# A gated-delta layer's head preparation: query scaling, query products and convolution rows one chunk later, absolute values on ScalarE

## What is computed

```python
qkv, new_buf = _causal_conv(qkv, buf, conv_w)       # 4 taps, then silu
q = _l2norm(q) * (GDN_DK ** -0.5)
k = _l2norm(k)
# per chunk: M = I + strict(beta * k k^T * decay), u and w by M^-1
Aqk = jnp.einsum('nbhtk,nbhsk->nbhts', q, k) * decay
def step(S, inp):
    v_new = uc - jnp.einsum('bhtk,bhkv->bhtv', wc, S)
    o = einsum(qc, S) + einsum(ac, v_new)
    S = glc[..., None, None] * S + jnp.einsum('bhsk,bhkv->bhkv', kc, v_new)
o = _rmsnorm(o, out_norm) * jax.nn.silu(g)           # g is z in the kernel
```

## Time and profile before

| | |
|---|---|
| median of 3 runs | 2057.86 us (2053.31 to 2070.72) |
| the profiled execution | 2055.79 us, its span 2054.0 us |
| busy: PE, PEld | 1845.4 us (90%), 1746.1 us (85%) |
| busy: DVE, ACT, POOL | 1142.2 us (56%), 530.3 us (26%), 543.7 us (26%) |
| mean granted clock of PE | 0.922 of full speed |
| chain that ended last | PE 42%, DVE 5%, ACT 4% of the span; L489 28% |
| GDN heads 0 to 7 | about 977 to 1600 us of the span |

### The profile page before, as it was taken

How to read it: one execution, slowest core, us unless ns; L and a number is a source line. 1 busy time by engine, 2 the same in 40 slices (tenths; PEclk the granted TensorE clock), 3 DMA queues, 4 the chain that set the end, 5 groups by cost and what they waited for, 6 DMA issues and landing times.

```text
span 2054.0 us, 34009 instructions
## 1 busy us (share of the span) xinstructions
PE 1845.4 (90%) x13227; PEld 1746.1 (85%) x13227; DVE 1142.2 (56%) x1824; ACT 530.3 (26%) x991; POOL 543.7 (26%) x303
## 2 busy tenths in 40 slices
PE   3999999979999999977988888888978899999997
PEld 3988888869999999976877778777757899999996
DVE  5677777758625252766456555556542771616263
ACT  1544445421000000114334434434421110100011
POOL 1100000006656565641000000000000565656562
PEclk9989999989999999987988988999966999999997
DMA  5122222212323222221120120120110223232321
GB/s 167 52 63 63 63 67 68 63 55 83 93 83 93 82 84 84 83 63 26 50 65 22 44 64 20 44 64 21 43 44 1 84 83 92 84 90 84 89 84 43
DMA packets 257434, 135.99 MB, mean 66 GB/s; under 512 B 6698, under 2 KB 255876, under 8 KB 257348
## 3 DMA queue, kind: packets, MB, share of 16 engines
q1 hardware_dynamic: 219700, 114.03, 19.5%
q10 hardware_dynamic: 37648, 20.68, 3.5%
HBM read 122.70 MB, written 12.00 MB: 66 GB/s over the span
## 4 chain that ended last, share of the span: by engine, by line
PE 42%; DVE 5%; ACT 4%; issue 3%; ACTq 0%; POOL 0%; DVEq 0%; POOLq 0%
PE pj L489 28%; PE rr L527 3%; PE rr L763 2%; PE rr L739 2%; PE rr L510 1%; DVE pr L1607 1%; PE rr L755 1%; PE rr L748 1%; PE rr L832 1%; PE rr L820 1%; PE rr L684 1%; DVE ol L1824 1%; ACT ws L1086 1%; ACT w_hi L945 1%; ACT ng L1079 1%
## 5 line engine op out<-in xcount | busy, mean ns | idle before, releaser
L450 POOL TENSOR_SCALAR w_hi<-w_raw 128x1024 fp32r<-128x1024 f32 x149 | 157.3, 1056 | 1464.2 <-PE pj L489 1433.4
L489 PE MATMUL pj<-xh,w_hi 128*128 128x272 f32 x2064 | 472.5, 311 | 23.4 <-DVE xl L1372 9.1
L489 PE MATMUL pj<-xh,w_lo 128*128 128x272 f32 x2064 | 443.7, 298 | 0.0
L489 PE MATMUL pj<-xl,w_hi 128*128 128x272 f32 x2064 | 443.4, 298 | 0.0
L452 POOL TENSOR_TENSOR w_lo<-w_raw,w_hi 128x1024 fp32r<-128x1024 f32 x149 | 386.1, 2591 | 12.5
L489 PEld LDWEIGHTS pj<-xh,w_hi 128*128 128x128 f32 x2064 | 339.4, 199 | 47.1 <-issue 23.9
L489 PEld LDWEIGHTS pj<-xl,w_hi 128*128 128x128 f32 x2064 | 341.9, 198 | 4.0 <-issue 4.0
L489 PEld LDWEIGHTS pj<-xh,w_lo 128*128 128x128 f32 x2064 | 340.3, 198 | 0.0
L489 PE MATMUL pj<-oh,w_hi 128*128 128x272 f32 x1280 | 271.1, 293 | 16.9 <-DVE ol L1402 5.4
L489 PE MATMUL pj<-oh,w_lo 128*128 128x272 f32 x1280 | 267.0, 290 | 0.0
L489 PE MATMUL pj<-ol,w_hi 128*128 128x272 f32 x1280 | 266.7, 290 | 0.0
(11 more groups left out here) (273 smaller groups left out, 2279.6 us busy)
## 6 DMA issues: line engine op xcount, KB each, us to landing
w_raw<-in_mlp_w_up_dram SPq DMA_DIRECT2D x64, 512.0 KB, 4.0
w_raw<-in_mlp_w_down_dram SPq DMA_DIRECT2D x64, 512.0 KB, 3.7
w_raw<-in_hgrn_w_in_dram SPq DMA_DIRECT2D x32, 512.0 KB, 4.0
w_raw<-in_gdn_w_in_dram SPq DMA_DIRECT2D x32, 512.0 KB, 4.2
out_dram<-S ACTq DMA_DIRECT2D x16, 512.0 KB, 3.3
S<-in_state_hgrn_dram ACTq DMA_DIRECT2D x8, 512.0 KB, 4.0
w_raw<-in_hgrn_w_out_dram SPq DMA_DIRECT2D x8, 512.0 KB, 3.7
S<-in_state_gdn_dram ACTq DMA_DIRECT2D x8, 512.0 KB, 4.2
```

The lines of the kernel that those rows point to most:

```text
L450: nc.gpsimd.tensor_scalar(w_hi[:, s], w_raw[:, j], 1.0, 1.0, ALU.mult, ALU.mult).then_inc(hi_pool, 1)
L489: last = mm(pj[:, s, b, 0:HALF], w[:, s, k, :], v[:, k, b * HALF:(b + 1) * HALF], start=(k == 0 and a == 0), stop=(k == KT - 1 and a == 2))
```

## The change

In program order on each engine:

- DVE loses the four `negative_abs` of a head. ACT's `soft` takes the convolved rows themselves and makes three activations of them, `Abs`, `Exp` with scale −1, and `Ln`.
- DVE: `nl` moves from C2 to C0, `qn` from C0 to C1 (behind z's evacuation), `qkd` from C1 to a new slot C3, which runs after the last state. `low(U_GIN+5)` moves from c = 0 to c = 1.
- ACT: `high(U_GIN+5)` moves from c = 0 to c = 1, behind z's exponential and logarithm; `zsig` stays in C2; `cout` and the stores move to C3, behind the copy and the square of the output (`oo`, `sq`), with `high(U_GIN+6)` behind them.
- PE: `qk` moves from C1 to C2, `stash` from C2 to C3, behind `dSs0` and two tiles. One of the three last tiles moves ahead of `gdn_first_inverse`.

```diff
-                if slot == "C1":
+                if slot == "C2":
                     pe.wait_ge(v.sem, v.after("qn", h))
                     for c in range(NC):
                         cols = slice(c * P, (c + 1) * P)
                         mm(rr[:, 2 + c // 2, c % 2 * P:(c % 2 + 1) * P], nK[:, cols], nQ[:, cols], start=True, stop=True)
                     t.did(mm(rr[0:TS, 3, 2 * P:2 * P + TS], nK[:, TP:T], nQ[:, TP:T], start=True, stop=True), "qk")
-                if slot == "C2":
+                if slot == "C3":
                     held((v, "qkd", h))
...
-                    if nxt is not None:
+                    if nxt is not None and c < NC - 1:
                         gdn_prepare(f"C{c}", nxt)
                 pe.wait_ge(v.sem, v.after("S3", h))
                 t.did(mm(rr[:, 0, :], kdTs[:], gd_vbig[0], start=True, stop=True), "dSs0")
                 later(2)
                 if nxt is not None:
+                    gdn_prepare("C3", nxt)
+                    later(1)
                     pe.wait_ge(s.sem, s.after("oo", h))
                     gdn_first_inverse(nxt, (sa, "cout", nxt))
                 pe.wait_ge(v.sem, v.after("sn0", h))
                 t.did(mm(rr[:, 0, :], kdTs[:], gd_vbig[1], start=True, stop=True), "dSs1")
-                later(3)
+                later(2)
...
-            def soft(row, w, exp, ln):
+            def soft(name, row, w, h):
 
                 s = st["ga"][1]
-                s.did(f(ng[:, row, 0:w], ng[:, row, 0:w], ACT.Exp), exp[0])
-                sem_of(s, *exp)
-                s.did(f(ng[:, row, 0:w], ng[:, row, 0:w], ACT.Ln, bias=1.0), ln)
+                s.did(f(ng[:, row, 0:w], pr[:, row, 0:w], ACT.Abs), f"{name}abs")
+                sem_of(s, f"{name}abs", h)
+                s.did(f(ng[:, row, 0:w], ng[:, row, 0:w], ACT.Exp, scale=-1.0), f"{name}exp")
+                sem_of(s, f"{name}exp", h)
+                s.did(f(ng[:, row, 0:w], ng[:, row, 0:w], ACT.Ln, bias=1.0), f"{name}ln")
...
-                    sem_of(v, "qneg", h)
-                    soft(1, YW, ("qexp", h), "qln")
+                    sem_of(v, "q3", h)
+                    soft("q", 1, YW, h)
...
-                    sem_of(v, "zneg", h)
-                    soft(2, T, ("zexp", h), "zln")
+                    act.wait_ge(unit_out, h * 4 + (U_GIN + 3 + 3))
+                    soft("z", 2, T, h)
                 if slot == "C2":
+                    sem_of(v, "zls", h)
+                    s.did(f(ng[:, 2, 0:T], ng[:, 2, 0:T], ACT.Exp), "zsig")
+                if slot == "C3":
...
-                    sem_of(v, "zls", h)
-                    s.did(f(ng[:, 2, 0:T], ng[:, 2, 0:T], ACT.Exp), "zsig")
...
-                    if nxt is not None:
+                    if nxt is not None and c < NC - 1:
                         gdn_prepare(f"C{c}", nxt)
-                        if c == 0:
+                        if c == 1:
                             high(nxt, U_GIN + 5)
-                        if c == NC - 1 and not final:
-                            high(nxt, U_GIN + 6)
                 sem_of(t, "o", h)
                 s.did(f(oo[:, 0:TP], rr[:, 1, :], ACT.Copy), "oo")
                 sem_of(s, "oo", h)
                 s.did(f(sqr, oo, ACT.Square), "sq")
+                if nxt is not None:
+                    gdn_prepare("C3", nxt)
+                    if not final:
+                        high(nxt, U_GIN + 6)
...
-                    after(v, f"{name}3", h)
-                    v.did(negative_abs(row, YW), f"{name}neg")
...
-                    after(s, "rnq", h)
-                    v.did(stt(out=nQ, in0=nQ, scalar=float(P) ** -0.5, in1=G, op0=ALU.mult, op1=ALU.mult), "qn")
-                if slot == "C1":
-                    tt(halves(pr[:, 2, 0:T]), computed(U_GIN, h * 4, 3), halves(rstd[:]), ALU.mult).then_inc(unit_out, 1)
-                    dve.wait_ge(unit_out, h * 4 + (U_GIN + 3 + 3))
-                    v.did(negative_abs(2, T), "zneg")
-                    after(t, "qk", h)
-                    decayed(3, "qkd")
-                if slot == "C2":
                     after(v, "kkd", h)
                     tt(blocks(gd["NL"][:, 0:TP], P), blocks(work[:, 0:TP], P), over_chunks(cf[:, C_NSTR:C_NSTR + P]), ALU.mult)
                     v.did(tt(gd["NL"][0:TS, TP:T], work[0:TS, TP:T], cf[0:TS, C_NSTRS:C_NSTRS + TS], ALU.mult), "nl")
+                if slot == "C1":
+                    tt(halves(pr[:, 2, 0:T]), computed(U_GIN, h * 4, 3), halves(rstd[:]), ALU.mult).then_inc(unit_out, 1)
+                    after(s, "rnq", h)
+                    v.did(stt(out=nQ, in0=nQ, scalar=float(P) ** -0.5, in1=G, op0=ALU.mult, op1=ALU.mult), "qn")
+                if slot == "C2":
                     after(s, "zln", h)
                     v.did(log_sigmoid(2, T), "zls")
+                if slot == "C3":
+                    after(t, "qk", h)
+                    decayed(3, "qkd")
...
-                        if c == 0:
+                        if c == 1:
                             low(nxt, U_GIN + 5)
```

More of the change, by code:

```diff
@@ L52 @@
 Q_ROW, K_ROW, V_ROW = 0, 1, 2
-GDN_SLOTS = ["L0", "L1", "L2x", "L2", "L3x", "L3", "L4x", "L4", "L5x", "L5", "L6x", "L6", "C0", "C1", "C2"]
+GDN_SLOTS = ["L0", "L1", "L2x", "L2", "L3x", "L3", "L4x", "L4", "L5x", "L5", "L6x", "L6", "C0", "C1", "C2", "C3"]
 SRT = 352
@@ L236, in build @@
             gp=["x", "neg", "ls", "g", "g2", "scan", "dl"],
-            ga=["cols", "gsel", "k1", "k2", "k3", "kneg", "kls", "q1", "q2", "q3", "qneg", "dec", "ks", "qls", "kn", "kb",
-                "v1", "v2", "v3", "vneg", "qs", "kkd", "vls", "vs", "qn", "zneg", "qkd", "nl", "zls", "tt0", "tt1", "A",
+            ga=["cols", "gsel", "k1", "k2", "k3", "kls", "q1", "q2", "q3", "dec", "ks", "qls", "kn", "kb",
+                "v1", "v2", "v3", "qs", "kkd", "vls", "vs", "nl", "qn", "zls", "qkd", "tt0", "tt1", "A",
                 "qe", "cols2", "nbe"],
@@ L253, in build @@
             gp=["A", "exp", "ln", "be", "el", "eg", "cols"],
-            ga=["hist", "past", "ktap", "qtap", "vhist", "kexp", "kln", "G", "ksig", "qexp", "qln", "bb", "dec",
-                "sqk", "vtap", "qsig", "lnk", "rnk", "eG", "sqq", "vexp", "vln", "vsig", "lnq", "rnq", "zexp", "zln", "cout",
-                "zsig", "K", "tm0"],
+            ga=["hist", "past", "ktap", "qtap", "vhist", "kabs", "kexp", "kln", "G", "ksig", "qabs", "qexp", "qln", "bb", "dec",
+                "sqk", "vtap", "qsig", "lnk", "rnk", "eG", "sqq", "vabs", "vexp", "vln", "vsig", "lnq", "rnq",
+                "zabs", "zexp", "zln", "zsig", "cout", "K", "tm0"],
             gr=["x2", "tt2", "x4", "tt4", "x8", "tt8", "x16", "tt16", "x32", "rs", "tt32", "vns", "x64", "os",
@@ L1110, in gdn_prepare @@
                 if slot == "L3":
-                    sem_of(v, "kneg", h)
-                    soft(0, YW, ("kexp", h), "kln")
+                    soft("k", 0, YW, h)
                 if slot == "L4x":
@@ L1140, in gdn_prepare @@
                 if slot == "L6":
-                    sem_of(v, "vneg", h)
-                    soft(0, YW, ("vexp", h), "vln")
+                    sem_of(v, "v3", h)
+                    soft("v", 0, YW, h)
                 if slot == "C0":
```

## The result

The changed kernel takes **2083.46 us** (median of 7 runs, 2077.59 to 2087.25) against 2064.54 us for the kernel before (7 runs beside them). The medians differ by 19 us; the ratio is 1.0106, 95% interval 1.007 to 1.0141, which makes it slower by about 22 us. The forecast was +10 us. The profiled execution took 2087.25 us (span 2085.4, mean clock 0.915; before 2055.79, 2054.0 and 0.922), 31 us more than the one of before.

What follows compares the result with a forecast made beforehand. TensorE's own work, its stalls and the half clock bound a head. Six heads at +2.2 (walk +1.5, levels +0.7) make +13.2, plus 0.35, less 3.6: +10 us on 2055.8, so 2066 us, range 2042 to 2084.

Steps and rivals of the forecast that it cites:

- rival (d): Levels' added 0.70 us brings 1.7 us more half clock in seven heads, both tiles stay half clock: 2076 to 2088, chance 0.22.
- The levels, +0.70 us per head: Absolute values on ACT: k and v cost nothing, q's delays `x32` and `dt32` by 0.70 us in seven heads.
- The walk up to dSs0: Chunks 0 to 3: `vn1` 2.2 us earlier, `vn2` 1.65 after a 3.6 us stall, `vn3` 2.36; 1.2 half clock after `vn2`.
- From dSs0 to the next head: End of the walk: `dSs1` stalls 4.4 us for `sn0`, starting at 1138.0 against 1138.44, then two tiles.
- the half clock ending inside, 4.25: After `sn0`: `dSs1` 2.0 us, one tile about half clock, 2.0 + 0.75 + 1.5 = 4.25 us, making +0.3 instead of −1.4.
- the upper bound of +3.0: Per head, with half clock through both last tiles: +1.1 + 1.2 + 0.7 = +3.0 us; +18 us over six heads.
- I take 0.6 per head off for it, −3.6: Deduction over six heads, since a head of another length than the 78.55 us ones meets the half clock elsewhere.
- Head 0's preparation, 0: Gains 0.67 (v's absolute value off DVE before `sqq`), loses 0.64 (`stash` behind a later `qkd`): 0.
- Head 6, +0.35: Head without tile or `high(U_GIN+6)`: `dSs1` 0.35 us forward, with the levels' +0.70 it is +0.35 us.
- Rival (c): ACT's two issues or DVE's order do not hold `sn0`, the 4.4 us stall falls away: 2030 to 2040, chance 0.08.

Runs made afterwards that it cites:

- the two pads: The changed kernel with idle ACT copies behind q's logarithm in every head, one of 544 columns or four of 128: 2080.39 and 2084.76 us.
- `high6_back`: The changed kernel with `high(U_GIN+6)` back in its old place on ACT, right behind the last chunk's copy: 2040.15 us.
- `both`: The changed kernel with `high(U_GIN+5)` ahead of z's three activations and `high(U_GIN+6)` back behind the last chunk's copy: 2021.39 us.
- `moves_only`: The changed kernel with all four absolute values back on DVE, the moves kept: 2080.96 us, ratio 1.0103 to the kernel before.

## Why the prediction was right in direction and too small

The measured time lies 0.5 us inside the stated range and in the interval of rival (d). The stalls came as forecast, and the sum made too little of them: one term was too small and one had the wrong sign.

**The levels, +0.70 us per head: right.** The wait before `dt32` is 1.04 us, and from the next head's first matmul behind the projections (L510) to `vn0` it takes 0.72 us longer. So k and v cost nothing, as said.

**The walk up to dSs0: right.** From `vn0` (1111.65 before, 1122.63 after), `vn1` comes 2.41 us earlier (said 2.2), `vn2` 1.61 (said 1.65), `vn3` 1.14 (said 2.36 less 1.2 of half clock, 1.16), `dSs0` 1.39 (said 2.84 less 1.2).

**From dSs0 to the next head: mis-sized, by 1.3 us a head.** `dSs1` comes 28.15 us behind `vn0` instead of 26.61, +1.54; the sum had −0.44 + 1.2 = +0.76. `cout` starts 3.27 us behind `dSs0`, where 2.8 was taken, and `dSs0` itself was 0.25 us later than said. From `cout` on it is 5.58 us against 5.7. A last 0.18 is that the old `dSs1` was read at 1138.44 in the chain, where the timeline has 1138.26. Then "the half clock ending inside, 4.25" failed: from `dSs1` to the first matmul of the next head it is 4.80 us, with `dSs1` and nearly all of the twelve matmuls at half clock. The walk is +2.8 us instead of +1.5, and a head +3.5 instead of +2.2. That is above the upper bound of +3.0, too. Six heads make +21, and the fit over all runs has +21.3 at equal half clock.

A check was at hand in the prediction's own numbers. Its stalls add up to 3.6 + 4.4 + 0.7 against 2.23 + 1.95, +4.5 us of standing in each head; with a head of +2.2 TensorE would have to be busy 2.3 us less. It was busy 0.83 us less.

**"I take 0.6 per head off for it, −3.6": wrong in sign.** I took the heads of 78.55 us for unlucky ones, which any change of length would on average help. For a pad in the kernel before that is true (−59 us of half clock). For this change it is not: the first five heads all have 18 to 21 us of half clock in the profiled execution, and the two pads win none. The two intervals which before took 74.38 and 75.90 us, with 10.4 and 13.6 us of half clock, now have 19.2 and 20.7 and take 81.44 and 82.13. Over all runs the changed kernel has 343 us of half clock against 330, so in place of −3.6 this term is about +5 (0.40 × 13 us). That the two long stalls are what keeps the half clock is argued from `high6_back` (295 us), which removes one, and `both` (277 us), which removes it and cuts the other to 1.0 us; it is not shown apart from the place of the heads.

With both put right the sum is 21 + 0.5 + 5 = 27 us, against 22 by the ratio and 31 between the profiled executions.

**Head 0's preparation, 0: +0.1. Head 6, +0.35: +0.5, in part by luck.** In head 6 `dSs1` was to come 0.35 us earlier against `vn0` and comes 1.95 earlier (21.88 us behind it, 23.83 before); 7.3 us more half clock in that interval (27.1 against 19.8), and the late end of the head before it, fill the place. The +2.8 us ahead of the heads are in no step. The same matmuls took longer there, with 10 us more half clock; the change has no part in that stretch, and runs of one kernel differ by more.

**The rivals.** The time fell into (d)'s interval, and the second half of (d) came true: both tiles stay at half clock nearly to the end, 0.55 us above the 4.25 of the sum. The reason that (d) gave first didn't. The extra half clock lies in the heads that had been shorter before, not in one more stretch behind q's absolute value, and `moves_only` loses nearly as much as the whole change. (The terms of (d), 7 × 1.7 + 6 × 0.8, make 16.7 us and not 12.) Rival (c) fell: `high` starts at 1147.81, behind the stores' issue at 1145.90 + 1.80. But it named the right lever: with the stores behind, 19 us come back, and with `high` back in its place 43.

## What to carry to other kernels

When a step moves along an in-order queue, look for what becomes queued behind it, its DMA issues included: here two `high` of 1 us each, for which another engine's queue waits, were put behind three activations and behind two store issues, and a good move cost 1% where it could win 1.8%. Add up the stalls of a head before and after first: here they grew by 4.4 us and the head by 3.55. Then price the half clock over all the work behind a stall, and don't count on luck: the first five heads of the changed kernel, with stalls of 3.5 and 4.4 us, all had 18 to 21 us of it, and those of the kernel before, with stalls of 2 us, had 10 to 21. And before a tuned kernel serves as a base for small changes, try a pad in it: if an idle 0.6 us makes it faster, differences of 1% may tell of its place against the clock rather than of the change.

## What was not expected of the hardware

A copy of 0.6 us that nothing needs, in each of eight heads, takes 1.1% (some 23 us) off the kernel before, with 59 us less half clock; its own executions, unpadded, spread over 41 us. The time follows the half clock at 0.40 us per us over all runs here. Two gaps of 2.67 and 1.56 us within 4 us of each other went with a clock of 0.51 over 13.64 us, although TensorE was busy for 12.35 of these, while the one gap of 4.37 us in the changed kernel went with 0.50 over 6.60 us.
